# Sample stage of a fused decoder step: order of page loads, units of background work, matmul shapes, and a split last tile

## The chip, the cores and the metric

The kernel is one launch on one core of a Trainium2 chip. The time is the device time of that launch in microseconds; of several runs the median is given.

## What is computed

One layer for a prompt group (512 tokens) and a sample group (8 sequences of 8 new tokens with 1024 past positions in a paged cache), with shared weights. The part that the change touches, cut from the reference:

```python
# state-space branch (output side)
y = einsum('gcp,btgp->btgc', c_re, x_re) - einsum('gcp,btgp->btgc', c_im, x_im) + d * u
y = gelu(y.reshape(b, t, 512))
y_lin, y_gate = split(y @ w_glu, 2)
ssm_out = (y_lin * sigmoid(y_gate)) @ w_ssm_proj

# compression of cached keys and values, blocks of 32 rows with stride 16
hidden = gelu(lead[:, :-1] + trail[:, 1:] + pe_term + b1);  kc = hidden @ w2

# attention of the sample tokens: compressed blocks, selected blocks, window
o = gate[0] * o_c + gate[1] * o_s + gate[2] * o_w

# merge of the branches, then norm, router, experts
x = x + (sigmoid(g_s) * ssm_out + sigmoid(g_a) * (o @ w_attn_proj)) @ w_out
y = x + hier_moe(rms_norm(x, g_ffn))
```

The selection keeps 16 of 17 blocks, so the kernel masks the one block with the least score. Everything is float32.

## The kernel before

The program runs seven phases with a barrier of all engines between them: projection, building the state-space matrices, prompt attention, sample, merge, experts, combine. The change touches sample and merge.

**Sample.** The 8 sequences go two at a time through a loop of 4 iterations p. Each iteration on TensorE is: wide scores against window and cached keys (L1301 to L1308), the compressed keys and values (L1317, L1320), their scores (L1328), the sum over heads and the transposed probabilities (L1334, L1335), the compressed product (L1341), the compression of the next iteration's pages (`compress`, L1279), transposes of the probabilities (L1355) and two products with values, window then selected (L1373). ScalarE and VectorE evacuate, take softmaxes and run the selection, a chain of small VectorE steps (L1584 to L1604) between the head sum and the selected probabilities.

Between these steps stand nine points per iteration at which TensorE issues background work from a list that `background()` writes: state-space output units ("y", L1223 with 128 rows and L1225 with 64 rows, 8 of them, into PSUM banks 6 and 7), their transposes ("t", L1235), gated units ("g", L1246, 8 units of two halves e, each half an entry of its own) and the projection ("p", L1257, 16 of them). The work of entry n is evacuated by ScalarE and VectorE in `back_out(n + 1)`, a y unit's second half in `back_out(n + 2)`. START = 5 entries come ahead of the loop, entries behind point 36 after it. All y units are elementwise gelu on the way out: square (L1399), two VectorE steps (L1520, L1521), tanh (L1392), two VectorE steps (L1510, L1512).

Pages: SyncE issues one DMA per page of 128 KB, 16 per iteration, for the compressed slots into `pgc` (L1149; half of iteration 0 by ScalarE); GpSimd issues the other slots. `pgc` is single, so the pages of iteration p + 1 wait until `compress(p)` has read it (`cmp_ps`). SyncE also loads window keys and values (L1180, L1183), w_glu and w_ssm (L1186, L1187), which lie over matrices that the y units read, and the gates `sig_s` (L1193), all in one program order.

**Merge.** The attention projection (L1716), then for 5 row tiles (4 of 128 rows, the last of 64) the output projection in two halves of 512 columns (L1727, `out_ps`), the sum with x (L1806), the norm (L1774 to L1811), transposes (L1737) and router logits (L1743). Then the routing on VectorE and the expert loop, whose weights stream in: six pieces, 12 MB, are fetched ahead in merge, and each later one when the matmuls have used up its buffer.

## Time and profile before

| | |
|---|---|
| median of 3 runs | 1377.42 us (1375.86 to 1383.63) |
| profiled execution | 1375.69 us, span 1374.0 us |
| TensorE matmul | 1087.0 us busy, 79% of the span |
| VectorE, ScalarE, GpSimd | 391.6, 268.2, 236.5 us |
| mean granted clock | 0.876 |
| HBM | 284.27 MB read, 25.58 MB written |

From the page, the busy tenths in 40 equal slices of 34.35 us:

```profile
PE   5999997977789747789899966988778777777760
DVE  4446441657752322224342142000000000000005
PEclk9999998668875757889999976999999999999995
DMA  8321253130005044243065032999999999999946
```

Slices 13 to 20 are the sample stage, up to slice 24 merge and routing, then the expert loop. In timelines "idle before" is the time in which the engine did nothing ahead of the instruction, with what released it. Times are us from the start of the span.

### The profile page before, as it was taken

To read this page: it belongs to the slowest core of one execution; us is meant where nothing else is said; L and a number is where in the kernel's file an instruction comes from. 1 tells how busy PE (TensorE), PEld (TensorE's weight loads), DVE (VectorE), ACT (ScalarE), POOL (GpSimd) and SP (SyncE) were. 2 spreads that over 40 slices of the span, in tenths; PEclk is the share of its full clock that TensorE was granted. 3 is DMA by queue.
4 is the path that set the end of the run, shared out by engine and by line. 5 is a ranking of instruction groups with operands and counts; after the bars stand their busy time and mean duration, and the time that the engine had idled before them with its cause. 6 is when DMAs were issued, how large, how long until landed. Compare 5 with 4: busy or idle time off the path is not lost. (4 is left out here: it accounts for less than half of the span.)

```text
span 1374.0 us, 16631 instructions
## 1 busy us (share of the span) xinstructions
PE 1087.0 (79%) x5930; PEld 681.3 (50%) x5930; DVE 391.6 (29%) x957; ACT 268.2 (20%) x567; POOL 236.5 (17%) x604
## 2 busy tenths in 40 slices
PE   5999997977789747789899966988778777777760
PEld 5999997853346535557674433333222223223220
DVE  4446441657752322224342142000000000000005
ACT  5423222334431102111101110110100001111012
POOL 0007922088504001020000001010000000000010
PEclk9999998668875757889999976999999999999995
DMA  8321253130005044243065032999999999999946
GB/s 333 108 92 63 87 183 89 38 134 1 5 0 189 27 184 163 75 154 146 1 265 216 26 141 104 421 421 420 421 421 421 421 422 421 421 421 421 420 195 221
DMA packets 71256, 299.30 MB, mean 218 GB/s; under 512 B 12086, under 2 KB 30390, under 8 KB 44694
## 3 DMA queue, kind: packets, MB, share of 16 engines
q1 hardware_dynamic: 60750, 274.79, 50.5%
q0 software_dynamic: 9296, 22.71, 4.6%
q10 hardware_dynamic: 1152, 1.05, 0.3%
q8 instruction: 34, 0.56, 0.2%
q14 instruction: 24, 0.20, 0.0%
HBM read 284.27 MB, written 25.58 MB: 226 GB/s over the span
## 5 line engine op out<-in xcount | busy, mean ns | idle before, releaser
L2020 PE MATMUL ps<-arena,local_late 128*64 128x512 f32 x1280 | 308.5, 630 | 99.7 <-DMA arena<-in_w_exp 80.6
L2020 PEld LDWEIGHTS ps<-arena,local_late 128*64 128x64 f32 x1280 | 101.7, 144 | 294.8 <-issue 273.1
L349 PE MATMUL ps<-local_project 128*128 128x288 f32 (+4 forms) x1608 | 205.2, 290 | 17.6 <-DVE local_project L488 16.8
L349 PEld LDWEIGHTS ps<-local_project 128*128 128x128 f32 (+1 forms) x1608 | 204.3, 184 | 18.1 <-DVE local_project L488 16.8
L2068 DVE SCALAR_TENSOR_TENSOR arena<-arena,ps 128x512 f32<-128x512 f32 x16 | 11.0, 688 | 306.6 <-ACT arena L2052 306.6
L1149 POOL DMA_DIRECT2D local_sample<-in_cache x64 | 35.1, 549 | 215.2 <-issue 215.2
L1727 PE MATMUL ps<-local_late,arena 128*128 128x512 f32 (+1 forms) x160 | 69.6, 594 | 1.0 <-DVE arena L1797 1.0
L1990 POOL TENSOR_TENSOR arena<-arena 1x1 f32<-1x1 f32 x16 | 2.9, 183 | 350.4 <-ACT local_late L2060 350.4
L2044 ACT ACTIVATE local_late<-ps 128x512 f32<-128x512 f32 x34 | 18.5, 594 | 221.3 <-PE ps L2003 221.3
L1246 PE MATMUL ps<-arena 128*128 128x288 f32 x128 | 43.1, 490 | 18.5 <-DVE arena L1526 18.5
L2071 DVE SCALAR_TENSOR_TENSOR arena<-arena,ps 128x512 f32<-128x512 f32 x16 | 11.0, 688 | 163.9 <-PE ps L2020 163.9
L2020 PE MATMUL ps<-local_late 128*64 128x512 f32 x256 | 57.7, 592 | 0.0
L389 DVE TENSOR_TENSOR local_project<-arena,local_project 128x2048 fp32r<-128x2048 f32 (+1 forms) x15 | 35.4, 2361 | 66.5 <-ACT local_project L301 66.5
L1279 PE MATMUL ps<-arena 128*128 128x128 f32 x256 | 33.7, 299 | 18.8 <-DMA arena<-in_cache 18.8
L1727 PEld LDWEIGHTS ps<-local_late,arena 128*128 128x128 f32 (+1 forms) x160 | 28.4, 179 | 39.5 <-issue 37.9
L891 PE MATMUL ps<-local_prompt 64*128 64x128 f32 (+3 forms) x128 | 31.1, 581 | 19.8 <-ACT local_prompt L951 18.9
L1279 PEld LDWEIGHTS ps<-arena 128*128 128x128 f32 x256 | 33.0, 214 | 20.0 <-DMA arena<-in_cache 19.2
L1246 PEld LDWEIGHTS ps<-arena 128*128 128x128 f32 x128 | 27.7, 227 | 28.1 <-DVE arena L1526 19.9
L2060 ACT ACTIVATE local_late<-ps 128x512 f32<-128x512 f32 x32 | 19.1, 597 | 105.5 <-PE ps L2020 105.5
L1257 PE MATMUL ps<-arena 128*128 128x288 f32 x128 | 35.1, 424 | 3.5 <-DVE arena L1533 3.5
L1970 POOL MEMSET arena<- 1x8 f32 x1 | 0.1, 95 | 217.8 <-POOLq L2208 217.8
L951 ACT ACTIVATE local_prompt<-ps,local_prompt 128x128 f32<-128x128 f32 (+3 forms) x64 | 33.0, 521 | 21.8 <-DVE local_prompt L1007 21.7
(377 smaller groups left out, 1405.4 us busy)
## 6 DMA issues: line engine op xcount, KB each, us to landing
arena<-in_w_exp SPq DMA_DIRECT2D x160, 1024.0 KB, 25.3
local_late<-in_w_exp SPq DMA_DIRECT2D x32, 1024.0 KB, 25.5
arena<-in_w_rest SPq DMA_DIRECT2D x9, 1024.0 KB, 5.7
local_sample<-in_cache POOLq DMA_DIRECT2D x64, 128.0 KB, 3.1
arena<-in_cache SPq DMA_DIRECT2D x56, 128.0 KB, 3.8
arena<-in_w_wide SPq DMA_DIRECT2D x6, 1040.0 KB, 5.2
scratch_sig<-arena POOLq DMA_DIRECT2D x16, 288.0 KB, 2.6
arena<-scratch_sig SPq DMA_DIRECT2D x2, 2304.0 KB, 9.5
```

What stands on the lines that cost most here:

```text
L349: mm = pe.matmul(out, stationary(s, k), moving(m, k), start=k == 0 and a == 0, stop=k == KD - 1 and a == 2)
L389: dve.tensor_tensor(W[:, n % 2, 1, :, 0:width], raw[:, n % 2, :, 0:width], W[:, n % 2, 0, :, 0:width].bitcast(F32), ALU.subtract).then_inc ...
L891: mm = pe.matmul(c.ps[:, t % 2 * 2 + g, 0:n], qT[HD * g:HD * (g + 1), h, i * P:(i + 1) * P], kT[HD * g:HD * (g + 1), s, 0:n], start=True, ...
L951: ins = act.activation(pr[:, s, g, h, 0:n], c.ps[:, t % 2 * 2 + g, 0:n], ACT.Exp, bias=bias[:, t % 4, g:g + 1], scale=-1.0, accum_out=tota ...
L1149: eng.dma_start(dst[:, a], c.d["cache"][bass.ds(v, 1)].rearrange("o p s e -> (o p) s e")[:, parts]).then_inc(arrived, 16)
L1246: mm = pe.matmul(c.ps[:, 6 + e, 0:HALF], w_glu[:, k, (4 * e + j) * P:(4 * e + j + 1) * P], yT[:, k, t], start=k == 0, stop=k == 3)
L1257: mm = pe.matmul(c.ps[:, 6 + u % 2, 0:HALF], w_ssm[:, k, m * P:(m + 1) * P], glu[:, k, t], start=k == 0, stop=k == 3)
L1279: mm = pe.matmul(c.ps[:, 4, (s * 2 + g) * P:(s * 2 + g + 1) * P], c.w1[:, s, j], mov, start=j == 0, stop=j == 7)
L1727: mm = pe.matmul(c.ps[0:ROWS[i], n, :], sig_a[:, k, i * P:i * P + ROWS[i]], w_out[:, k, n * 512:(n + 1) * 512], start=k == 0, stop=k == KD ...
L2020: mm = pe.matmul(c.ps[SLOTS * q:SLOTS * (q + 1), bank, :], tokens[:, k0 + k, SLOTS * q:SLOTS * (q + 1)], raw[p][q][:, k], start=first and ...
L2044: act.activation(XT[:, 4 * a:4 * a + 4], c.ps[:, a, :].rearrange("p (k t) -> p k t", k=4), ACT.Copy).then_inc(xt_out, 1)
L2060: act.activation(Y[:, h * 512:(h + 1) * 512], c.ps[:, 6 + h, :], ACT.Copy).then_inc(y_out, 1)
```

## The change

- The background list has 4 y units instead of 8, each with both halves (64-row parts side by side in two banks, banks 6/7, 0/1, 2/3, 6/7), and whole gated units at every other entry instead of halves at every entry. The second (gate) half comes first, so that ScalarE can start on it.
- The order ahead of the loop is y 0, y 1, compression 0, y 2, y 3.
- Y units are evacuated whole in `back_out(n + 1)`; for VectorE one `back_out` moves into the selection chain, ahead of the masking.
- SyncE loads the pages of iteration 1 ahead of w_glu and w_ssm, and window keys and values of iteration 1 ahead of the gates.
- The compression multiplies 256 columns at once instead of twice 128.
- In merge, the last row tile's two column halves go to different output partitions (0 to 63 and 64 to 127) of two banks, alternating; ScalarE copies the second half down to partitions 0 to 63 before VectorE adds it.

```diff
-    y = [[("y", n)] for n in range(8)]
+    y = [[("y", n)] for n in range(4)]
     turn = [[("t", n), ("t", n + 1)] for n in range(0, 8, 2)]
-    glu = [[("g", u, e)] for u in range(8) for e in range(2)]
+    glu = [part for u in range(8) for part in ([("g", u)], [])]
...
+        Y_BANK = [6, 0, 2, 6]
...
-            pages(sp, 0, pgc, slice(0, 2), cmp_in, range(PAGES))
-            for p in range(NP):
+            def window(p):
                 if p:
                     sp.wait_ge(wide_ps, p)
                 sp.dma_start(wk[:], c.d["win_kT"][:, 2 * p:2 * p + 2]).then_inc(wk_in, 16)
                 if p:
                     sp.wait_ge(pv_ps, 3 * (p - 1) + 2)
                 sp.dma_start(wv[:], c.d["win_v"][:, 2 * p:2 * p + 2]).then_inc(wv_in, 16)
-                if p == 0:
-                    sp.wait_ge(y_ps, 8)
-                    sp.dma_start(w_glu[:], c.d["w_glu"]).then_inc(wg_in, 16)
-                    sp.dma_start(w_ssm[:], c.d["w_ssm"]).then_inc(ws_in, 16)
-                if p + 1 < NP:
-                    sp.wait_ge(cmp_ps, p + 1)
-                    pages(sp, p + 1, pgc, slice(0, 2), cmp_in)
-                if p == 0:
-                    sp.wait_ge(yt_ps, 8)
-                    sp.dma_start(sig_s[:], c.d["sig"][0:8].rearrange("m p t -> p m t")).then_inc(ss_in, 16)
+
+            def next_pages(p):
+                sp.wait_ge(cmp_ps, p)
+                pages(sp, p, pgc, slice(0, 2), cmp_in)
+
+            pages(sp, 0, pgc, slice(0, 2), cmp_in, range(PAGES))
+            window(0)
+            next_pages(1)
+            sp.wait_ge(y_ps, 8)
+            sp.dma_start(w_glu[:], c.d["w_glu"]).then_inc(wg_in, 16)
+            sp.dma_start(w_ssm[:], c.d["w_ssm"]).then_inc(ws_in, 16)
+            window(1)
+            sp.wait_ge(yt_ps, 8)
+            sp.dma_start(sig_s[:], c.d["sig"][0:8].rearrange("m p t -> p m t")).then_inc(ss_in, 16)
+            for p in range(2, NP):
+                next_pages(p)
+                window(p)
...
-                        if u >= 2:
-                            pe.wait_ge(y_done, u - 1)
+                        if u == 1:
+                            pe.wait_ge(small_out, 3)
+                        if u == 3:
+                            pe.wait_ge(y_done, 2)
                         for a in range(4):
-                            g = 2 * (4 * (u // 2) + a) + u % 2
-                            lo, tl = HD * (g % 2), g // 2
-                            out = c.ps[0:NCH, 6 + u % 2, a * P:(a + 1) * P]
-                            pe.matmul(out, c.U[:, g], c.KT[:, :, g * 16:(g + 1) * 16], start=True, stop=False)
+                            out = [c.ps[0:NCH, Y_BANK[u] + h, a * P:(a + 1) * P] for h in range(2)]
+                            tl = 4 * u + a
+                            for h in range(2):
+                                g = 2 * tl + h
+                                pe.matmul(out[h], c.U[:, g], c.KT[:, :, g * 16:(g + 1) * 16], start=True, stop=False)
                             for r in range(2):
-                                mm = pe.matmul(out, c.XM[lo:lo + HD, r, tl], c.C[lo:lo + HD, r, tl].rearrange("p t e -> p (t e)"),
-                                               start=False, stop=r == 1)
-                        mm.then_inc(y_ps, 1)
+                                for h in range(2):
+                                    rows = slice(HD * h, HD * (h + 1))
+                                    mm = pe.matmul(out[h], c.XM[rows, r, tl], c.C[rows, r, tl].rearrange("p t e -> p (t e)"),
+                                                   start=False, stop=r == 1)
+                                    if a == 3 and r == 1:
+                                        mm.then_inc(y_ps, 1)
...
-                        e, j, t = unit[2], u // 2, slice(u % 2 * HALF, (u % 2 + 1) * HALF)
-                        if u == 0 and e == 0:
+                        j, t = u // 2, slice(u % 2 * HALF, (u % 2 + 1) * HALF)
+                        if u == 0:
                             pe.wait_ge(yt_out, 8)
                             pe.wait_ge(wg_in, 16)
-                        if u >= 1 and e == 0:
+                        else:
                             pe.wait_ge(glu_done, u)
-                        for k in range(4):
-                            mm = pe.matmul(c.ps[:, 6 + e, 0:HALF], w_glu[:, k, (4 * e + j) * P:(4 * e + j + 1) * P],
-                                           yT[:, k, t], start=k == 0, stop=k == 3)
-                        mm.then_inc(glu_ps, 1)
+                        for e in (1, 0):
+                            for k in range(4):
+                                mm = pe.matmul(c.ps[:, 6 + e, 0:HALF], w_glu[:, k, (4 * e + j) * P:(4 * e + j + 1) * P],
+                                               yT[:, k, t], start=k == 0, stop=k == 3)
+                            mm.then_inc(glu_ps, 1)
...
-                    for g in range(2):
-                        for j in range(8):
-                            mov = pgc[:, :, s].rearrange("p a (g j n) -> p a g j n", g=2, j=8)[:, :, g, j]
-                            mm = pe.matmul(c.ps[:, 4, (s * 2 + g) * P:(s * 2 + g + 1) * P], c.w1[:, s, j], mov,
-                                           start=j == 0, stop=j == 7)
+                    out = c.ps[:, 4, s * 2 * P:(s + 1) * 2 * P].rearrange("p (g a n) -> p a g n", g=2, n=8)
+                    for j in range(8):
+                        mov = pgc[:, :, s].rearrange("p a (g j n) -> p a g j n", g=2, j=8)[:, :, :, j]
+                        mm = pe.matmul(out, c.w1[:, s, j], mov, start=j == 0, stop=j == 7)
...
-            for n in range(START - 1):
+            back_step(0)
+            back_step(1)
+            compress(0)
+            for n in range(2, START):
                 back_step(n)
-            compress(0)
-            back_step(START - 1)
             pe.wait_ge(small_out, 3)
             pe.wait_ge(qb_zero, 9)
+            pe.wait_ge(y_done, 6)
...
+                        for h in range(2):
+                            act.wait_ge(y_ps, 2 * u + h + 1)
+                            if u:
+                                act.wait_ge(y_tanh, 2 * u + h - 1)
+                            act.activation(tmp[0:NCH, h, 0], c.ps[0:NCH, Y_BANK[u] + h, :], ACT.Square).then_inc(sq_done, 1)
+                        for h in range(2):
+                            act.wait_ge(u_ready, 2 * u + h + 1)
+                            if u:
+                                act.wait_ge(y_done, 2 * u + h - 1)
+                            act.activation(tmp[0:NCH, h, 1], tmp[0:NCH, h, 0], ACT.Tanh, scale=GELU_B).then_inc(y_tanh, 1)
...
-            for n in range(START - 1):
+            for n in range(2):
                 back_out(n)
             for g in range(2):
                 r = slice(HD * g, HD * (g + 1))
                 for h in range(HG):
                     act.activation(qb[r, :, g, h], qs[r, h].rearrange("p (b t) -> p b t", b=NB), ACT.Copy).then_inc(qb_zero, 1)
-            back_out(START - 1)
+            back_out(2)
             trail_rows(0)
             hidden_tanh(0)
+            for n in range(3, START):
+                back_out(n)
...
-            for n in range(START):
+            for n in range(3):
                 back_out(n)
             hidden(0)
+            for n in range(3, START):
+                back_out(n)
...
                 link(dve.tensor_scalar(b17[:, 3], b17[:, 2], s1[:, 13:14], NEG, ALU.is_equal, ALU.mult))
+                back_out(point(p, 3))
...
-                for k in range(3, 7):
+                for k in range(4, 7):
...
-                if i < TILES:
+                if i < TILES - 1:
                     for n in range(2):
                         if i >= 1:
                             pe.wait_ge(x_done, 2 * i + n - 1)
@@ -1727,6 +1745,14 @@
                             mm = pe.matmul(c.ps[0:ROWS[i], n, :], sig_a[:, k, i * P:i * P + ROWS[i]],
                                            w_out[:, k, n * 512:(n + 1) * 512], start=k == 0, stop=k == KD - 1)
                         mm.then_inc(out_ps, 1)
+                if i == TILES - 1:
+                    pe.wait_ge(x_done, 2 * i)
+                    for k in range(KD):
+                        for n in range(2):
+                            mm = pe.matmul(c.ps[64 * n:64 * (n + 1), n, :], sig_a[:, k, SEQ:TOK],
+                                           w_out[:, k, n * 512:(n + 1) * 512], start=k == 0, stop=k == KD - 1)
+                            if k == KD - 1:
+                                mm.then_inc(out_ps, 1)
...
+                if i == TILES - 1:
+                    act.wait_ge(out_ps, 2 * TILES)
+                    act.activation(moved[:], c.ps[64:P, 1, :], ACT.Copy).then_inc(half_moved, 1)
...
-                    dve.tensor_tensor(xs, c.ps[0:r, n, :], xs, ALU.add).then_inc(x_done, 1)
+                    term = c.ps[0:r, n, :]
+                    if i == TILES - 1 and n == 1:
+                        dve.wait_ge(half_moved, 1)
+                        term = moved[:]
+                    dve.tensor_tensor(xs, term, xs, ALU.add).then_inc(x_done, 1)
```

The evacuation of a y unit on VectorE has the same steps as before, for h = 0 and h = 1, and counts `y_ps`, `u_ready`, `y_tanh` and `y_done` by halves.

## Rows read from the trace of the kernel before

**Rows 1.** Busy time by stage: stretch, length, then busy time (instructions), clock, DMA.

```profile
414.40:689.40 275.00, 214.58 (x1206) 156.66 (x1206) 84.15 (x228) 45.57 (x127) 35.11 (x64) 0.78 0.34 117
689.40:840.80 151.40, 124.55 (x448) 75.14 (x448) 49.05 (x121) 14.40 (x29) 4.22 (x7) 0.89 0.38 149
840.80:1374.00 533.20, 394.53 (x1786) 149.35 (x1786) 42.02 (x57) 62.55 (x114) 45.33 (x98) 0.92 0.94 386
```

**Rows 2.** Groups by line and shape, whole kernel: busy, mean ns, idle before.

```profile
L1246 PE MATMUL ps<-arena 128*128 128x288 f32 x128 | 43.1, 490 | 18.5 <-DVE arena L1526 18.5
L1257 PE MATMUL ps<-arena 128*128 128x288 f32 x128 | 35.1, 424 | 3.5 <-DVE arena L1533 3.5
L1279 PE MATMUL ps<-arena 128*128 128x128 f32 x256 | 33.7, 299 | 18.8 <-DMA arena<-in_cache 18.8
L1225 PE MATMUL ps<-arena 64*72 64x128 f32 x128 | 33.2, 406 | 0.0
L1223 PE MATMUL ps<-arena 128*72 128x128 f32 x64 | 20.5, 420 | 8.1 <-DVE arena L1512 8.1
L1235 PE MATMUL ps<-arena 72*128 72x72 f32 x32 | 4.5, 312 | 4.9 <-ACT arena L1403 2.5 <-DVE arena L1512 2.4
```

**Rows 3.** SyncE's waits in 410 to 680 us: total, times, longest.

```profile
SPq L1186 <- PE ps L1225: 64.3, 1, 64.3
```

**Rows 4.** Timeline of SyncE's queue: start, duration of issuing, instruction.

```profile
488.79 0.33 SPq L1186 DMA_DIRECT2D arena<-in_w_glu  x1
...
490.35 17.26 SPq L1149 DMA_DIRECT2D arena<-in_cache  x16
533.03 0.40 SPq L1193 DMA_DIRECT2D arena<-scratch_sig  x1
533.47 0.58 SPq L1180 DMA_DIRECT2D arena<-in_win_kT  x1
...
587.79 16.85 SPq L1149 DMA_DIRECT2D arena<-in_cache  x16
```

**Rows 5.** Timeline of TensorE: start, busy, instruction, idle before.

```profile
453.26 0.38 PE L1223 MATMUL ps<-arena 128*72 128x128 f32 x2
...
457.02 0.34 PE L1301 MATMUL ps<-local_sample 128*64 128x64 f32 x4
...
509.45 9.19 PE L1279 MATMUL ps<-arena 128*128 128x128 f32 x64 [18.81 <-DMA arena<-in_cache]
...
543.81 0.42 PE L1301 MATMUL ps<-local_sample 128*64 128x64 f32 x4 [4.45 <-issue]
...
565.97 4.21 PE L1246 MATMUL ps<-arena 128*128 128x288 f32 x8 [6.19 <-DVE arena L1526]
...
677.72 9.97 PE L1257 MATMUL ps<-arena 128*128 128x288 f32 x40
```

**Rows 6.** Timeline of TensorE in prompt attention, 64-row scores on alternating row halves.

```profile
371.63 1.99 PE L891 MATMUL ps<-local_prompt 64*128 64x512 f32 x8
```

**Rows 7.** Busy time and clock of two stretches, columns as in rows 1.

```profile
416.00:443.00 27.00, 27.00 (x98) 17.12 (x99) 8.10 (x20) 5.62 (x17) 12.79 (x24) 0.50 0.71 224
...
640.00:660.00 20.00, 19.16 (x127) 12.80 (x125) 11.09 (x35) 3.58 (x14) 0.00 (x0) 1.00 0.54 216
```

**Rows 8.** Timeline, evacuation of a y unit: its first and last step.

```profile
423.88 0.59 ACT L1399 ACTIVATE local_sample<-ps 72x512 f32<-72x512 f32 x1
...
427.94 0.69 DVE L1512 TENSOR_TENSOR arena<-ps,local_sample 72x512 f32<-72x512 f32 x1
```

**Rows 9.** Timeline of the last row tile in merge and of the first experts.

```profile
787.83 13.95 PE L1727 MATMUL ps<-local_late,arena 128*64 128x512 f32 x32
...
801.81 0.68 DVE L1806 TENSOR_TENSOR arena<-ps,arena 64x512 f32<-64x512 f32 x1 [6.18 <-PE ps L1727]
...
806.51 0.97 PE L1737 MATMUL ps<-arena,local_late 64*128 64x64 f32 x8 [1.00 <-DVE local_late L1811]
...
844.76 15.39 PE L2020 MATMUL ps<-arena,local_late 128*64 128x512 f32 x64 [1.37 <-ACT local_late L2044]
```

50 lines of the change are left out of this document (19 added, 31 removed).

## Prediction

> **What bounds the kernel now.** I read the busy table by stage first. The sample stage (414.4 to 689.4 us) lasts 275.0 us with TensorE busy for 214.6 of them, the merge stage 151.4 us, and the expert loop with the tail 533.2 us at 386 GB/s, DMA share 0.94 [rows 1]. The last of these is bound by reading expert weights: its length does not depend on when it begins, since its transfers start only as its own matmuls release buffers, and the six pieces that are fetched ahead are fetched in merge. So a microsecond taken from sample or merge is a microsecond of the whole, and in both TensorE is the engine that everything follows. The second view, the groups by line with shapes kept apart, says what its 275 us are: gated units (L1246) 43.1 us busy and 18.5 idle before them, projections (L1257) 35.1 and 3.5, compression (L1279) 33.7 and 18.8, state-space output (L1225 and L1223) 33.2 + 20.5 = 53.7 and 8.1, its transposes (L1235) 4.5 and 4.9, and the wide scores (L1301) have 4.45 before them [rows 5]. Together these are 58 of the 60.4 us in which TensorE is idle. The third view is the clock: 0.50 through the first 27 us of state-space output although TensorE never paused, and 1.00 in 640 to 660 us [rows 7]. A projection group of 8 instructions costs 9.97 / 5 = 1.99 us at the full clock, and the same shape 4.21 us in the stretch that follows a 6.19 us pause [rows 5].
>
> **The change, part by part.**
>
> *Pages ahead of weights.* SyncE stands 64.3 us until the last state-space unit is out [rows 3]. Only then, at 488.79 us, do w_glu and w_ssm go out and, behind them, the 16 pages of iteration 1, at 1.05 us of issuing each (17.26 us) [rows 4]. TensorE wants them at 490.6 and gets them at 509.45: 18.8 us idle [rows 2, 5]. The change lets these pages go when compression 0 has ended (about 444 us, below), so they are issued by 461 and are there before compression 1 can start (477). The 18.8 us go entirely. What is late next is the chain of small steps ahead of compression 1. The window keys of iteration 1 are now issued before the gates: before, they stood behind 2.3 MB of gates (533.03, 533.47) and landed for a start at 543.81, so these 4.4 us go too [rows 4, 5]. New on SyncE: the wait for the window product of iteration 0 (window values 1) now holds back the gates and the pages of iteration 2. It ends at about 492 by my walk, pages 2 are in by 515, and compression 2 wants them at about 523: hidden by 8 us. Pages 3 start after the window product of iteration 1, as before (587.79) [rows 4], but the iterations are shorter: about 2 to 4 us of cover are left. That is a rival.
>
> *State-space output in row halves.* A unit now holds both halves: 16 instructions over 128 rows and 32 over 64 rows, where before two units held the same 48. The halves sit on different rows and in different banks. The row for such pairs is the prompt's 64-row scores: 8 instructions of 512 columns in 1.99 us, 0.25 each [rows 6], where 512 columns alone cost 13.95 / 32 = 0.44 each [rows 9]. So 32 cost what 16 did: 32 instruction times a unit in place of 48. An instruction time is 53.7 / 192 = 0.28 us on average, nearly all at half clock [rows 2], and (457.02 - 453.26) / 24 = 0.157 at full clock [rows 5]. Two units before compression 0 at half clock, 9.0 us each, and two behind it at full clock, 5.0 each (before, the clock was full behind compression 0 too), give 28 in place of 53.7 us: -25.7. Bounds: no pairing gives 13.5 and 7.5, so 14 us more; full clock from the start, 8 us less. The 8.1 us of waits for banks 6 and 7 go, as units 1 and 2 write banks 0 to 3. In their place stands one wait: evacuating a unit, from square to product, took 423.88 to 428.63 for one half [rows 8], some 5.5 us for two, and transposes and score reads stand behind that of unit 3: 3 us idle beside the wide scores.
>
> *Turns inside iteration 0.* The 8 transposes now lie in the softmax chain of iteration 0 where four output units lay, and alternate with ScalarE's copies, which stand behind that iteration's own ScalarE work. By walking the three queues instruction by instruction compression 1 starts at 477 (before 509.45), with about 4 us idle among them, near the 4.9 us that they had [rows 2]. The last two copies stand behind the trail rows of compression 1, so the first gated unit waits 2 us.
>
> *Whole gated units, cleared mid-chain.* Work is unchanged: 16 groups of gating, 16 of projection, 1.99 us each at the full clock, 31.8 us a kind. Before, 43.1 + 35.1 were spent; the excess of 14.6 is slow clock behind pauses [rows 2]. The pauses of 18.5 come from a unit whose clearing lay behind the selection chain of VectorE (6.19 the longest [rows 5]). A unit is now issued only at every other point, so its clearing has a whole point to itself, and for the projections the one before is cleared inside the chain. What remains: about 1 us at each score read, 2 at the softmax of iterations 0 and 1 where no group covers it any longer, 1 for the product with its predecessor: 4.3 us in iteration 1, 2 in iteration 2, 1.5 in 3, 2.8 in the rest of 0. As eight y units became four, the background list ends inside iteration 3: the four projections behind the loop (of 9.97 us for five [rows 5]) move into iterations 0 to 2 and are no longer alone at the end. Slow clock: I leave 2 of the 14.6 in place for gating and none for projection, and add 5 us below for it.
>
> *Compression 256 wide.* 32 instructions in place of 64 for the same columns. At full clock 128 columns cost about 0.116, and 288 columns 9.97 / 40 = 0.249, so 256 should cost 0.22: 0.4 us saved each time, -1.7 together. The loads were hidden already. A dearer pattern of reading is not seen in any row; bounds -2 and +3.
>
> *Last tile split.* The 64 rows of tile 4 took 13.95 us for 32 instructions [rows 9]. With its two halves on different columns they should run as the experts' do, 64 in 15.39 us, 0.24 each [rows 9]: 7.7 us, -6.2. Both halves now end together, so the added copy (a similar one took 0.59 [rows 8]) and one sum that was hidden (0.68 [rows 9]) stand on the path, and the copy behind tile 3's evacuation: about 4.4 of the 6.2 reach the start of the last transposes at 806.51 [rows 9]. Bounds: -5.5 and, if the columns don't pair, +1.4.
>
> *The sum.* Busy: output 28, gating 34, projection 32, compression 32, and the rest, 214.6 - 53.7 - 43.1 - 35.1 - 33.7 = 49.0, about 46: 172 us. Idle: start 1.7, output 3, turns 4, rest of iteration 0 4.8, iterations 4.3 + 2 + 1.5, end 2: 23. With 5 for slow clock behind the new short pauses: 200 us. The walk along the order of instructions, with each semaphore's own delay, gives 208. I take 206: -69. With the tile -73. The profiled execution is 1375.7 us (span 1374.0) against a median of 1377.4; 1377.4 - 73 = 1304.
>
> **The rivals.**
>
> *Output units dearer than priced* (1317): pairs don't form or loads show, 8 to 14 us more. Against it stands the prompt's row [rows 6]; for it, that the 64-row pairs there are 4 times as wide. The Trainium skill, "TensorE: Matmul & The Clock Gate", Part 3, says both that matmuls on different row groups run together and that a weight load overlaps only matmuls of other row groups. By the second half, the 16 full-height loads of a unit would stand open; whatever loads stand open in the kernel before already lie inside my 0.28 us, and my bound of 14 us holds the rest.
>
> *Pages 3 late* (1314): compression 3 waits on a queue that issues 16.85 us of pages [rows 4] in an iteration that has become 17 us shorter; 5 to 12 us, with the slow clock that follows a pause. By the Trainium skill, "DMA: Bandwidth & Descriptors", Issuing engines are not separate DMA queues, issuing is usually small beside the transfer; the row says the opposite here, 1.05 us to issue 128 KB. If the page held, this rival would have no chance.
>
> *Fuller clock* (1291): with fewer pauses the clock rises in the first output units and stays up: 8 us from output, 5 from my allowance.
>
> *Slower than before* (1400): the stage runs at half clock. The new order bunches transposes and short products in iteration 0 and leaves whole points uncovered; if the clock then stayed at 0.50, the 150 us of the sum that I price at full would double (4.21 for 1.99 [rows 5]). The change breaks even when some 70 of the 150 run so. Against it: 640 to 660 us, the same mix with pauses, stood at 1.00 [rows 7]; for it: 0.50 through 27 us of unbroken output [rows 7].
>
> *The time doesn't reach the end* (1350 to 1375): the expert loop waits for something that merge now reaches too early. The pieces fetched ahead are 12 of 1 MB in 151 us at 149 GB/s [rows 1], so there is room.
>
> **How the numbers follow.** Forecast 0.72, dearer output 0.09, late pages 0.07, fuller clock 0.07, slower 0.02, not reaching the end 0.03. The forecast's own range, from the bounds of compression (5), tile (6), pauses (8) and output (6), is 1292 to 1320. The range, which takes in the dear and the fuller case, is 1286 to 1331. A change under 0.5% can't be told from none here. Faster by more: 0.97; within: 0.01; slower: 0.02.
>
> **What would show it.** No idle before the compression of iteration 1; sample stage about 206 us; a state-space unit of 8 to 9 us at half clock and 5 at full; pauses before gated units under 5 us in all; the last projection before the loop's end; clock of the stage near 0.9; tile 4 in 7.7 us; expert loop and tail still 533 us. A long DMA-ended pause before compression 2 or 3, or a clock of 0.5 past 480 us, would make the prediction wrong.

## The result and the profile after

The kernel after takes 1284.22 us (median of 4 runs, 1283.38 to 1285.02), the kernel before 1376.64 us beside it (4 runs, 1375.79 to 1383.63). The ratio is 0.9316, 95% interval 0.9295 to 0.9337: 92 us or 6.8% faster. The forecast was 1304 us and its range ended at 1286, so the kernel came out 20 us faster than forecast and just below the range.

The busy table by stage of the kernel after (stretch, length, then busy time and instructions of TensorE, its weight loads, VectorE, ScalarE and GpSimd, the granted clock, the DMA share, GB/s), to be read against [rows 1]:

```profile
415.80:602.30 186.50, 167.35 (x1078) 124.39 (x1078) 83.17 (x228) 46.03 (x127) 35.02 (x64) 0.94 0.51 173
602.30:749.50 147.20, 118.71 (x452) 74.09 (x453) 49.07 (x121) 15.11 (x30) 4.22 (x7) 0.87 0.41 153
749.50:1283.30 533.80, 393.48 (x1784) 148.17 (x1782) 42.06 (x57) 62.55 (x114) 45.32 (x98) 0.93 0.94 385
```

The sample stage went from 275.0 to 186.5 us, merge from 151.4 to 147.2, and the expert loop with the tail, 533.8 us, kept its length and began earlier. With a start that is 1.4 us later, these make -90.7 us, which is the difference of the spans (1374.0 and 1283.3). In the sample stage TensorE's busy time fell by 47.2 us with 128 instructions fewer, all of them in compression, and its idle time fell from 60.4 to 19.2. The mean granted clock of the stage rose from 0.78 to 0.94.

The groups by line and shape (busy us, mean ns | idle before them), which answer to [rows 2]. L1271 is projection, L1260 gating, L1293 compression, L1237 and L1233 the state-space output over 64 and 128 rows:

```profile
L1271 PE MATMUL ps<-arena 128*128 128x288 f32 x128 | 36.3, 429 | 1.9 <-DVE arena L1547 1.1 <-DVE arena L1540 0.8
L1260 PE MATMUL ps<-arena 128*128 128x288 f32 x128 | 33.0, 411 | 4.3 <-DVE arena L1540 2.4 <-ACT arena L1416 2.0
L1293 PE MATMUL ps<-arena 128*128 128x256 f32 x128 | 30.5, 399 | 0.0
L1237 PE MATMUL ps<-arena 64*72 64x128 f32 x128 | 11.5, 302 | 0.0
L1233 PE MATMUL ps<-arena 128*72 128x128 f32 x64 | 11.4, 305 | 0.7 <-ACT arena L1467 0.7
```

State-space output is 22.9 us where it was 53.7, compression waits for nothing (18.8 before), gating waits 4.3 (18.5 before). Projection alone is no cheaper (36.3 for 35.1). A second profile of the same kernel (the yardstick below) has 36.4 us of gating in place of 33.0, at equal pauses, so 3.4 us of slow clock come and go there between executions.

TensorE's timeline from the first output unit to the first gated unit (start, busy, instruction, idle before it), which answers to [rows 5] and [rows 7]:

```profile
418.31 1.13 PE L1233 MATMUL ps<-arena 128*72 128x128 f32 x4
419.37 1.13 PE L1237 MATMUL ps<-arena 64*72 64x128 f32 x8
...
422.51 0.66 PE L1233 MATMUL ps<-arena 128*72 128x128 f32 x4
423.09 0.66 PE L1237 MATMUL ps<-arena 64*72 64x128 f32 x8
...
425.66 0.66 PE L1233 MATMUL ps<-arena 128*72 128x128 f32 x4 [0.72 <-ACT arena L1467]
...
430.37 7.17 PE L1293 MATMUL ps<-arena 128*128 128x256 f32 x32
...
451.84 0.72 PE L1248 MATMUL ps<-arena 72*128 72x72 f32 x8 [1.30 <-DVE arena L1532]
...
455.31 1.26 PE L1248 MATMUL ps<-arena 72*128 72x72 f32 x8 [1.20 <-ACT arena L1416]
...
461.33 1.27 PE L1248 MATMUL ps<-arena 72*128 72x72 f32 x8 [0.93 <-ACT arena L1416]
...
463.16 8.94 PE L1293 MATMUL ps<-arena 128*128 128x256 f32 x32
474.07 4.15 PE L1260 MATMUL ps<-arena 128*128 128x288 f32 x16 [1.96 <-ACT arena L1416]
```

Two things are to be seen. At 422.5 us, inside the first output unit, a group falls from 1.13 to 0.66 us: the clock has risen, where before it stayed at 0.50 for 27 us of the same work [rows 7]. And the 8 instructions of the 64-row group take what 4 of the 128-row group take, 1.13 us at half clock and 0.66 at full: the two halves run side by side. Compression 1 starts at 463.16, where before it started at 509.45 [rows 5]. The clock did not stay up all the way: among the turns, with pauses of 0.9 to 1.5 us, it was lower again (columns as in rows 1), and compression 1 began slow, 8.94 us for the 7.17 of compression 0.

```profile
451.80:463.10 11.30, 7.31 (x55) 5.98 (x55) 5.10 (x22) 5.12 (x13) 1.09 (x2) 0.56 0.88 308
```

SyncE's queue (start, duration of issuing), which answers to [rows 4]:

```profile
438.28 17.21 SPq L1149 DMA_DIRECT2D arena<-in_cache  x16
455.54 0.80 SPq L1193 DMA_DIRECT2D arena<-in_w_glu  x1
...
482.89 16.85 SPq L1149 DMA_DIRECT2D arena<-in_cache  x16
...
526.16 17.36 SPq L1149 DMA_DIRECT2D arena<-in_cache  x16
```

The pages of iteration 1 go out as compression 0 ends, and the weights behind them. The pages of iteration 3 are all issued at 543.5; compression 3 starts at 548.06 and waits for nothing.

The split tile, TensorE's timeline in merge, against [rows 9]:

```profile
700.71 7.09 PE L1752 MATMUL ps<-local_late,arena 128*64 128x512 f32 x32
...
714.09 1.11 PE L1763 MATMUL ps<-arena,local_late 64*128 64x64 f32 x8 [2.55 <-DVE local_late L1844]
```

From its first matmul to its last transposes it takes 13.4 us, where it took 18.7.

**Where the 20 us are.** I cut the sample stage of both traces at the same instructions:

| from .. to | before, us | after, us | change | prediction |
|---|---|---|---|---|
| start .. compression 1 | 95.0 | 47.3 | -47.7 | -32 |
| compression 1 .. wide scores of iteration 1 | 34.4 | 30.0 | -4.4 | not stated |
| iteration 1 | 55.8 | 38.8 | -17.1 | -17 |
| iteration 2 | 46.3 | 38.5 | -7.8 | not stated |
| iteration 3 and end | 43.5 | 31.9 | -11.6 | not stated |

The right-hand column holds what the prediction states of the walk that gave 208 us. Of the 21.5 us between 208 and the measured 186.5, about 16 lie in the first row: the walk was 8.8 us too dear in output units and compression 0, and 7.0 us too dear between the last output unit and compression 1. From compression 1 to compression 2 it had 46 us (477 to 523) and the trace has 46.8 (463.16 to 509.96), and iteration 1 came as it said. Where the other 5 or 6 us lie can't be told, as the prediction doesn't state its other parts.

### The profile page after: what moved, and what is told of

Read it like the earlier page. It is cut to its first block and busy times, and to the rows that moved or that the text cites. A ratio compares the mean times of both kernels' runs of the same rounds, so it can differ in the third digit from the quotient of the medians.

```text
span 1283.3 us, 16387 instructions
## 1 busy us (share of the span) xinstructions
PE 1033.2 (81%) x5802; PEld 647.7 (50%) x5802; DVE 391.0 (30%) x957; ACT 268.9 (21%) x568; POOL 236.5 (18%) x604
## 3 DMA queue, kind: packets, MB, share of 16 engines
q10 hardware_dynamic: 1152, 1.05, 0.3%
## 5 line engine op out<-in xcount | busy, mean ns | idle before, releaser
L349 PE MATMUL ps<-local_project 128*128 128x288 f32 (+4 forms) x1608 | 205.7, 290 | 18.0 <-DVE local_project L488 17.2
L349 PEld LDWEIGHTS ps<-local_project 128*128 128x128 f32 (+1 forms) x1608 | 204.7, 185 | 18.5 <-DVE local_project L488 17.2
L2077 ACT ACTIVATE local_late<-ps 128x512 f32<-128x512 f32 x34 | 18.4, 595 | 220.6 <-PE ps L2036 220.6
L1745 PE MATMUL ps<-local_late,arena 128*128 128x512 f32 x128 | 55.7, 594 | 1.0 <-DVE arena L1826 1.0
L1745 PEld LDWEIGHTS ps<-local_late,arena 128*128 128x128 f32 x128 | 24.1, 190 | 30.7 <-issue 29.2
L2085 ACT ACTIVATE arena<-ps 128x512 f32<-128x512 f32 x16 | 9.6, 597 | 137.5 <-PE ps L2053 137.5
L1271 PE MATMUL ps<-arena 128*128 128x288 f32 x128 | 36.3, 429 | 1.9 <-DVE arena L1547 1.1
L853 PEld LDWEIGHTS ps<-arena,local_prompt 128*128 128x128 f32 x160 | 23.9, 180 | 26.6 <-DVE local_prompt L982 13.8
L2053 PEld LDWEIGHTS ps<-local_late 128*64 128x64 f32 x256 | 18.6, 137 | 36.3 <-issue 36.1
L1260 PE MATMUL ps<-arena 128*128 128x288 f32 x128 | 33.0, 411 | 4.3 <-DVE arena L1540 2.4
L1007 DVE CUSTOM_DVE_ANT_0 ps<-ps,local_prompt 128x128 f32<-128x128 f32 (+3 forms) x64 | 30.2, 513 | 20.6 <-PE ps L891 20.4
```

The lines of the kernel that those rows point to most:

```text
L349: mm = pe.matmul(out, stationary(s, k), moving(m, k), start=k == 0 and a == 0, stop=k == KD - 1 and a == 2)
L853: mm = pe.transpose(c.ps[:, 4 + g, h * P:(h + 1) * P], pr[:, s, g, h, a * P:(a + 1) * P], c.k("ident"))
L1007: ins = dve.tensor_tensor_reduce(S, S, mask[:, SEQ - n:SEQ], -SCALE, 3.0e38, ALU.add, ALU.min, bias[:, t % 4, g:g + 1])
L1260: mm = pe.matmul(c.ps[:, 6 + e, 0:HALF], w_glu[:, k, (4 * e + j) * P:(4 * e + j + 1) * P], yT[:, k, t], start=k == 0, stop=k == 3)
L1271: mm = pe.matmul(c.ps[:, 6 + u % 2, 0:HALF], w_ssm[:, k, m * P:(m + 1) * P], glu[:, k, t], start=k == 0, stop=k == 3)
L1745: mm = pe.matmul(c.ps[0:ROWS[i], n, :], sig_a[:, k, i * P:i * P + ROWS[i]], w_out[:, k, n * 512:(n + 1) * 512], start=k == 0, stop=k == KD ...
```

## The experiments

Each kernel is the kernel after with one thing undone or varied, but for the third and fourth, which are the kernel before with one thing added. The edits are shown as sketches: `U, g` stands for the product over 128 rows, `XM, C of half h` for one over 64 rows, and lines that only follow the edit are left out. Times stand beside 1284.22 us of the kernel after, which gave 1284.41 in the third group of runs (the yardstick, below). The medians carry intervals of 0.15 to 0.4% of the kernel before, so a difference of 2 us between two kernels is not measured by its median; where one matters it is read from the timeline. The kernel before, run beside each group, had medians of 1376.6 to 1382.0 us, so the ratios compare better than the times. The start of the sample stage varies too, although nothing ahead of it was changed: the first output product starts between 414.7 and 420.9 us in these profiles. So timelines of two kernels are compared from that product on.

**1. The two halves one after the other.** Each half finishes its four tiles before the other starts; banks, places and waits stay.

```
-for a in range(4):
-    for h in range(2): U, g
-    for r in range(2):
-        for h in range(2): XM, C of half h
+for h in range(2):
+    for a in range(4):
+        U, g
+        for r in range(2): XM, C of half h
```

> The changed kernel with one edit: inside a state-space unit all products of the first half come ahead of all products of the second, so that no two neighbouring 64-row matmuls lie on different rows. Theory A (the pairs, and with them the denser work, raised the clock in the first unit): units 0 and 1 at the half clock as before the change, 13.4 us each, compression 0 about 9 us, units 2 and 3 7.6 us each behind it; the wide scores start 50 to 52 us after the first unit instead of 29.2; about 1306 us. Theory B (the clock rises in the first unit whatever the order, pairing only shortens the instructions): four units of 7.6 us and 7.2 for the compression, 37.6 us, about 1293 us. Theory C (pairing does nothing): as the changed kernel, 1284 us.

Measured: 1305.31 us, ratio 0.9472 (0.9457 to 0.9488), +21. Busy table and clock of units 0 and 1, and of units 2 and 3 behind compression 0:

```profile
417.00:444.00 27.00, 27.00 (x99) 17.12 (x98) 6.82 (x18) 4.88 (x16) 12.73 (x23) 0.50 0.70 224
454.30:469.30 15.00, 15.00 (x96) 9.87 (x95) 9.16 (x17) 4.21 (x8) 0.00 (x0) 1.00 0.39 114
```

The first 27 us are those of the kernel before to the microsecond, at 0.50 with TensorE busy without a pause. Behind compression 0 the same work runs at 1.00 in 15.0 us. So the order of the 48 instructions of a unit made the clock rise early. But the edit changes two things at once: the halves no longer stand side by side, and the shape changes four times a tile instead of twice. Experiments 10 to 12 take that up. One other explanation falls here: more instructions in the same time. The clock rose inside compression 0, between 448 and 450 us, and there TensorE had run 6 recorded instructions in 2 us (446 to 448), fewer in a microsecond than the 99 in 27 us of output.

**2. The weights ahead of the pages again.**

```
 window(0)
-next_pages(1)
 sp.wait_ge(y_ps, 8)
 ...w_glu, w_ssm
-window(1)
+next_pages(1)
 ...sig_s
+window(1)
```

> The changed kernel with SyncE's order of before: weights of the gated units ahead of the pages of iteration 1, gates ahead of the window of iteration 1. Theory A (the stall was the wait for the last state-space unit, not the weights' bytes): that unit now ends at 447, so the pages are issued 448 to 465 and compression 1 starts at about 467 instead of 463: +4 us, about 1288 us. Rival (the order itself was worth the stall of 18.8 us and the 4.4 us before the wide scores): +20 us or more, 1304 us or above.

Measured: 1291.75 us, 0.9369 (0.9351 to 0.9386), +7.5. TensorE's timeline:

```profile
470.21 8.05 PE L1293 MATMUL ps<-arena 128*128 128x256 f32 x26 [6.77 <-DMA arena<-in_cache]
```

The pages were late by 6.8 us, not by the 18.8 of before, as the four output units now end sooner. From the first output product to compression 1 it is 51.1 us, for 44.9 in the kernel after. The queue's order is worth some 7 us in the new kernel, more than the 4 that I expected, and the rival's 20 did not come.

**3. The pages ahead of the weights, alone, in the kernel before.** The new order of SyncE's queue, and nothing else.

> The kernel before with SyncE's new order alone. Theory A: the stall of 18.8 us and the 4.4 us before the wide scores of iteration 1 go and nothing takes their place: -23 us, about 1354 us; compression 1 starts at about 491. Rival (the evacuation of the last output units and the transposes behind it take part of the place of the stall): -12 to -18 us, 1359 to 1365 us.

Measured: 1349.93 us, 0.9789 (0.9773 to 0.9806), -27.8. The gated units of this kernel:

```profile
L1252 PE MATMUL ps<-arena 128*128 128x288 f32 x128 | 41.6, 477 | 18.5 <-DVE arena L1532 18.5
```

The wait before compression 1 is gone, and the pauses of gating are untouched, 18.5 us as in [rows 2]. I had priced the two stalls at 23.2 us. By the profiled spans the edit gives 25.4 (1374.0 to 1348.6), or 26.9 from the first output product on, which came 1.5 us later in this profile. Of the 3.7 us above the two stalls, 1.5 are gating at a fuller clock (43.1 to 41.6); where the rest lies I haven't followed.

**4. The paired output alone.** The kernel before with output in row halves and the shorter list of units; weights ahead of pages, gating in halves, nothing cleared mid-chain, compression 128 wide, last tile whole. Of the new gating only the order of the two halves is kept.

> The changed kernel with everything but the four double output units and their place reverted: SyncE's order, gated units by halves at every point, no clearing inside the selection chain, compression by 128 columns, last tile whole. Theory A (the units and the clock are the larger part): what is reverted costs 4 (order), 4.4 (tile), 1 (compression), 6 (gated units and clearing) us: about 1300 us. Rival (the whole gated units carry the 18.5 us of waits that stood before L1246): those come back, 1315 to 1320 us.

Measured: 1319.27 us, 0.9565 (0.9535 to 0.9594). Groups by line (L1259 is gating, L1270 projection), then the timeline at compression 1:

```profile
L1259 PE MATMUL ps<-arena 128*128 128x288 f32 x128 | 38.0, 443 | 18.4 <-DVE arena L1540 16.4 <-ACT arena L1416 2.0
L1270 PE MATMUL ps<-arena 128*128 128x288 f32 x128 | 36.9, 434 | 5.7 <-DVE arena L1547 3.5 <-DVE arena L1540 2.1
```

```profile
470.25 9.54 PE L1292 MATMUL ps<-arena 128*128 128x128 f32 x64 [6.79 <-DMA arena<-in_cache]
```

Of the 92 us, 58 come with this part. The shorter list does not take the pauses before gated units away (18.4 us), so it is the whole gated units that took them away (experiment 5). My theory, by which most of them would go with the list, fell here.

**5. Gating in halves, clearing mid-chain kept.**

```
-glu = [part for u in range(8) for part in ([("g", u)], [])]
+glu = [[("g", u, e)] for u in range(8) for e in (1, 0)]
```

> The changed kernel with gated units issued by halves at every point, as before the change, but with the clearing inside the selection chain kept. Theory A (the waits before L1246 came from a unit that is issued one point after its predecessor's second half, with the selection chain between them): the waits before gated units, 4.3 us now, return to 10 to 14 us, less than the 16.4 us of the run with no clearing in the chain, since the clearing now comes in its middle; about 1293 us. Rival (clearing in mid-chain alone cured them): waits stay under 6 us, 1285 us.

Measured: 1296.31 us, 0.9395 (0.9362 to 0.9428), +12.1.

```profile
L1259 PE MATMUL ps<-arena 128*128 128x288 f32 x128 | 40.0, 463 | 15.4 <-DVE arena L1539 13.5 <-ACT arena L1415 2.0
```

The pauses are back, a little above what I expected (15.4 for 4.3), and gating is busy 7.0 us longer (40.0 for 33.0). Some 5 of the 7 are slow clock in four groups of eight, the slowest 3.90 us for 2.21, each right behind a pause of 1.8 to 3.4 us. But 36.4 also occur in the kernel after, so how much of the 7 this edit brings is known to a few microseconds only. Projection is 1.7 us cheaper, which is the one slow group of the kernel after (3.90 for 2.21 at 541.64) at full clock.

**6. Nothing cleared mid-chain.** VectorE clears the unit of point 3 behind the selection chain again.

```
-back_out(point(p, 3))
 ...S, s1[:, 14:15], s1[:, 4:5]
-for k in range(4, 7):
+for k in range(3, 7):
```

> The changed kernel with the one clearing moved back behind the selection chain. Theory A (whole units at every other point never have their clearing behind the chain, only the projections of iteration 3 do): the wait of 3.5 us before a projection in iteration 3 returns in place of 1.1, about +2.5 us, 1287 us. Rival (the mid-chain clearing carries the gated units too): +8 us or more, 1292 us.

Measured: 1289.77 us, 0.9360 (0.9325 to 0.9395), +5.5, between the 2.5 that I expected and the rival's 8. Groups by line, then the timeline in iteration 3:

```profile
L1271 PE MATMUL ps<-arena 128*128 128x288 f32 x128 | 38.6, 450 | 4.3 <-DVE arena L1547 3.5 <-DVE arena L1540 0.8
```

```profile
585.09 4.21 PE L1271 MATMUL ps<-arena 128*128 128x288 f32 x8 [3.54 <-DVE arena L1547]
```

Gating is untouched (33.0 us busy, 4.3 idle): an empty point follows each gated unit, so its clearing needs no room inside the chain. What the edit costs is one pause of 3.54 us among the projections of iteration 3 and the clock behind it (4.21 for 2.21), which I had not priced. Iteration 3 is 5.0 us longer by it: 2.4 more idle before projections, 2.3 more busy in them, and a small rest behind them.

**7. The last tile whole.**

```
-if i < TILES - 1:
+if i < TILES:
```

(with the split branch, ScalarE's copy and its wait removed)

> The changed kernel with the last row tile whole. Both traces show 18.7 us from the tile's first matmul to the last transposes before the change and 13.4 us after it; so +5.2 us, about 1289.5 us. Rival (a neighbour of the tile gives it back: the router's chain or the row store ends last anyway): +0 to +2 us.

Measured: 1292.17 us, 0.9359 (0.9321 to 0.9396), +8.0. TensorE's timeline in merge:

```profile
706.65 13.95 PE L1745 MATMUL ps<-local_late,arena 128*64 128x512 f32 x32
...
725.34 0.73 PE L1755 MATMUL ps<-arena,local_late 64*128 64x64 f32 x8 [1.00 <-DVE local_late L1830]
```

13.95 us and 18.7 to the last transposes, as before: the split is worth 5.3 us. The rest of the 8 us is not the tile's. In this profile the tile begins 5.9 us later than in the kernel after, although nothing ahead of it was changed: 2.6 us of it are already there at the first output product, and 3.4 are gating, busy 36.4 us for 33.0. The yardstick, which is the kernel after itself, shows the same 36.4, in the same two units (5.84 us for 4.15, the first and the fourth). So the clock differs there between executions of one kernel; why stays open.

**8. Compression 0 behind all four output units.** It asks whether compression, the wide dense product, is what keeps the clock up for units 2 and 3.

```
-back_step(0); back_step(1); compress(0)
-for n in range(2, START): back_step(n)
+for n in range(START): back_step(n)
+compress(0)
```

> The changed kernel with compression 0 behind all four state-space units. Theory A (paired units alone raise and hold the clock): granted clock 1.0 in units 2 and 3 without a compression ahead of them, the four units end at about 440, the wide scores start where they did, and the pages of iteration 1, which wait for compression 0, come 9 to 10 us later, so compression 1 starts at about 467: +4 us, 1288 us. Theory B (the compression between them held the clock up): units 2 and 3 fall to 0.5 and take 8.4 us each instead of 4.7: +7 us more, 1295 us.

Measured: 1285.52 us, 0.9333 (0.9297 to 0.9370), +1.3. Busy table of units 2 and 3, then the timeline at compression 1:

```profile
427.00:440.00 13.00, 13.00 (x119) 9.83 (x116) 12.29 (x25) 7.92 (x20) 6.01 (x11) 1.00 0.53 183
```

```profile
463.79 8.40 PE L1293 MATMUL ps<-arena 128*128 128x256 f32 x29 [2.59 <-DMA arena<-in_cache]
```

The units ran at 1.00 with no compression ahead of them. The pages of iteration 1 wait for compression 0 and so arrive 2.6 us late. The stage began 2.7 us earlier in this profile; from the first output product to compression 1 it is 48.1 us, for 44.9 in the kernel after, so 3.3 us later, near the 4 expected. The median, +1.3, is too coarse for that.

**9. Compression 128 wide.**

```
-for j in range(8): out 256 wide, both g
+for g in range(2):
+    for j in range(8): out 128 wide
```

> The changed kernel with the compression by 128 columns. Four compressions of 64 instructions: at full clock 7.4 us instead of 7.17 each; +1 us in all, 1285 us, not to be told from the changed kernel by its time, only by the group's busy time (31.5 against 30.5 us). Rival (each dropped weight load was open): +3.7 us each, 1299 us.

Measured: 1285.98 us, 0.9318 (0.9286 to 0.9351), +1.6. All compression is busy 31.7 us there in 256 recorded instructions, and 30.5 us in 128 in the kernel after: the width is worth 1.2 us, for the 1.7 priced.

**The yardstick.** The kernel after once more, beside experiments 9 to 11.

> The changed kernel itself, again, as the yardstick of this chip: 0.9316 of the kernel before, stage of 186.5 us, first output unit at half clock for 4 us and all others at full.

Measured: 1284.41 us, 0.9311 (0.9285 to 0.9336). The group that differs from the profile shown at first:

```profile
L1260 PE MATMUL ps<-arena 128*128 128x288 f32 x128 | 36.4, 442 | 4.3 <-DVE arena L1540 2.4
```

The time is the same within its interval, though gating is busy 3.4 us longer.

**10. Only unit 0 in pairs.** Units 1 to 3 as in experiment 1.

> The changed kernel with paired products in state-space unit 0 only; units 1 to 3 in the unpaired order. Theory A (the pairs raise the clock, and once up it stays up in the unpaired order too, as it did for units 2 and 3 of the fully unpaired run): clock 1.0 from the first unit's second half on, units 1 to 3 cost 7.6 us each instead of 4.7, compression 0 7.2: +8.7 us, about 1293 us. Rival (the clock needs the pairs throughout): it falls back to 0.5 in unit 1, which takes 13 us, and compression 0 starts at half: +17 us or more, 1301 us.

Measured: 1290.81 us, 0.9358 (0.9334 to 0.9383), +6.4. Busy table of the first 5 us of unit 0, then of 27 us in which lie unit 1, compression 0 and most of units 2 and 3:

```profile
417.00:422.00 5.00, 5.00 (x29) 3.72 (x29) 0.00 (x0) 0.00 (x0) 2.41 (x5) 0.52 0.91 273
425.00:452.00 27.00, 27.00 (x159) 19.17 (x158) 18.41 (x40) 9.74 (x24) 13.06 (x24) 1.00 0.69 221
```

The clock rose inside unit 0 and the three unpaired units stayed at 1.00, without a pause. Once it is up, unpaired work keeps it; what experiment 1 lacked was the rise.

**11. The halves grouped.** Per tile both products over 128 rows, then both of the lower half, then both of the upper.

```
-for r in range(2):
-    for h in range(2):
+for h in range(2):
+    for r in range(2):
```

> The changed kernel with the 64-row products of a tile grouped by half: both 128-row products, then the two state products of the first half, then those of the second. The changes of shape are as few as in the changed kernel, but only one pair of neighbours per tile lies on different rows. Theory A (work side by side on both halves raised the clock): clock 0.5 through units 0 and 1, about 11 to 12 us each, compression 0 about 9: some +17 us, 1301 us. Theory B (fewer changes of shape, and so fewer pauses of the weight loads, raised it): clock 1.0 from unit 0 on, units of 5 to 6.5 us, +3 to +8 us, 1288 to 1292 us.

Measured: 1284.03 us, 0.9311 (0.9285 to 0.9338), the same as the kernel after. Busy table, then two groups of unit 0:

```profile
417.00:421.00 4.00, 4.00 (x24) 2.88 (x24) 0.00 (x0) 0.00 (x0) 2.07 (x4) 0.50 0.89 268
421.00:445.00 24.00, 23.71 (x203) 18.06 (x200) 17.48 (x39) 10.13 (x26) 11.06 (x21) 1.00 0.76 245
```

```profile
421.15 0.67 PE L1233 MATMUL ps<-arena 128*72 128x128 f32 x4
421.76 0.67 PE L1237 MATMUL ps<-arena 64*72 64x128 f32 x8
```

I had expected the halves to run one after the other here and the clock to stay low. It rose, and for a moment that spoke for the rival, fewer changes of shape. The rows say why it does not: 8 instructions of 64 rows still take 0.67 us, so the halves ran side by side all the same. Neighbours need not alternate strictly; the four instructions of the upper half ran beside the four of the lower that stood ahead of them. The experiment had not taken away what it was meant to.

**12. Same shapes, one half.** The alternation of the kernel after (two products over 128 rows, four over 64), but all four on the same half: two tiles take the place of the two halves. The results land in the places of other tiles, so this kernel doesn't compute the layer; it serves for its times alone. Units 0 and 2 do the lower half, units 1 and 3 the upper.

```
-tl = 4 * u + a; out[h]: half h of tile tl
+h = u % 2; tls = [8 * (u // 2) + 2 * b + i for i in range(2)]; out[i]: half h of tile tls[i]
```

> The kernel after, with the state-space output in the same alternation of shapes as there (two pieces of 128 rows, then four of 64 rows), but the four of 64 rows all on the same half: two tiles of the same half take the place of the two halves of one tile (units 0 and 2 do the lower half, units 1 and 3 the upper). The results land in the places of other tiles, so the output is not the reference's; the instructions are the same in number and shape. Theory A, the two halves side by side are what raised the clock: units 0 and 1 stay at 0.50, as in the unpaired kernel; a unit then takes 2 x 1.13 us for the 128 rows' and the 64 rows' blocks twice as long as in the kernel after (4 x (1.13 + 2.1) = 13 us), units 2 and 3 about 7.0 us each at full, and the kernel takes 1303 us or a little less. Theory B, fewer changes of shape raised it (two a tile instead of four): the clock rises inside unit 0 as in the kernel after (by 424), the 64 rows' blocks still take twice the time, 4 x (0.59 + 1.17) = 7.0 us a unit at full against 4.7, so 4 x 2.35 = 9.4 us more plus about 1 in the slow part: 1294 us. Busy time of the 64 rows' groups: 28 us or more by A, about 20 by B.

Measured: 1297.26 us, 0.9405 (0.9379 to 0.9431), +13.0. Busy table of units 0 and 1, and of units 2 and 3, then the timeline:

```profile
417.00:439.40 22.40, 22.40 (x92) 17.72 (x91) 5.70 (x16) 4.55 (x16) 10.39 (x20) 0.50 0.75 240
448.60:461.40 12.80, 12.80 (x97) 10.17 (x95) 8.04 (x15) 3.71 (x8) 1.64 (x3) 1.00 0.48 143
```

```profile
416.79 1.98 PE L1238 MATMUL ps<-arena 64*72 64x128 f32 x8
418.70 1.13 PE L1235 MATMUL ps<-arena 128*72 128x128 f32 x4
...
450.74 1.09 PE L1238 MATMUL ps<-arena 64*72 64x128 f32 x8
```

The shape changes exactly as often as in the kernel after, TensorE is busy without a pause, and the clock stays at 0.50 through both units. So the halves side by side raised the clock, not the grouping of shapes. The time alone would not have told: 1297 lies between the two expectations, because I had priced a unit at half clock at 13 us and it took 11.9. The clock column tells, and so does the time from the first output product to the wide scores: 45.7 us, for 29.2 in the kernel after and 51.5 in experiment 1. Of the 22 us between those two, 4 x (7.6 - 4.7) = 12 are the unpaired work at full clock, and the rest is the clock. What side by side changes that the clock answers to, a fuller array or more products in the same time, these runs don't separate.

**The parts add up.** Undone one at a time in the kernel after, the queue's order, whole gated units, mid-chain clearing, width and tile cost 7.5 + 12.1 + 5.5 + 1.6 + 8.0 = 34.7 us; experiment 4, which lacks all five, is 35.1 us above it. By ratios to the kernel before of the same group, the five make 31 us and experiment 4 34. With some 2 us of uncertainty in each of them, this leaves no room for a large interaction among the five. Pairing does interact, with the queue's order: together they removed the 18.8 us, of which the order alone would take all and pairing alone 12. No version tried is measurably faster than the kernel after.

## Why the prediction was right and where it was wrong

*What bounds the kernel: right.* A microsecond of the sample stage was a microsecond of the whole. Expert loop and tail took 533.8 us for 533.2 though they began 91 us earlier, and the case "the time doesn't reach the end" is out.

*Pages ahead of weights: right.* Both stalls are gone, none took their place, and experiment 3 gives 27 to 28 us for 23.2. In the whole kernel the order is worth 7 (experiment 2), because pairing takes 12 of the same 18.8 us. Pages 3 were all issued at 543.5, and a page takes a median of 3.0 us from issue to landing in this stage, so an estimated 1.5 us or more was left until 548.06, near the 2 to 4 that the prediction gave. The Trainium skill's page "DMA: Bandwidth & Descriptors", Issuing engines are not separate DMA queues, has issuing as usually small beside the transfer. Here 16 pages occupy SyncE for 17.2 us, 1.08 each (the prediction's 1.05 is that of the 16.85 us group): a third of the 3.0 us of one page. But the 16 transfers overlap and their issues don't, so issuing sets the time of the whole (in experiment 2 they were issued from 448.9 to 468.5, and compression 1 started at 470.2), and a queue's order remains worth watching.

*State-space output: mechanism right, size wrong, and this is the step that failed.* I priced two units at 9.0 us (half clock) and two at 5.0, 28 us, and compression 0 at half clock. The price at full clock was good (4.7 for 5.0). Wrong was the clause "two units before compression 0 at half clock". It rested on [rows 7], where the clock stood at 0.50 through the same products; but that row was taken with the halves one after the other, and the change ends just that. Units and compression 0 took 28.5 us (418.31 to 446.8) in place of 37.3 (2 x 9.0 + 9.3 + 2 x 5.0, with compression 0 at the 9.3 us of before), 8.8 less: 5.9 in units 0 and 1, 2.3 in compression 0, 0.6 in units 2 and 3. Experiments 1 and 12 show that side by side is the condition, 8 that compression is not, 10 that the clock then stays. The prediction's "fuller clock" rival had the mechanism ("the clock rises in the first output units and stays up: 8 us from output, 5 from my allowance"), and got a chance of 0.07. Its sizes are only near: 6.5 us came from output and 2.3 from compression 0, which it doesn't name, and the clock fell again among the turns (0.56 from 451.8 to 463.1).

*Turns inside iteration 0: the second mis-sized term.* The walk was given only by its result, 477. From the last output unit to compression 1 it was 16.3 us and not 23.3 (454 to 477). By my account, which the recorded prediction doesn't show, each of the eight turns of output stood in the walk at 1.27 us, which is what one entry of eight instructions takes: two turns. [rows 2] had the answer, 32 instructions in 4.5 us; 8 x 1.27 - 4.5 = 5.7 of the 7.0 are this. The idle time among them was about 5 us for the 4 given, and the first gated unit waited 1.96 for 2.

*Gating, projection, clearing.* Gating was 33.0 us for 34 and all its pauses with those of projection 6.2 us; experiment 5 shows the cause as the prediction has it. Projection was priced too low: 36.3 for 32. Of the 4.3, 1.7 are one slow group (3.90 for 2.21 at 541.64). The rest is the price itself: 1.99 us is the mean of five groups in a row, and a group that stands among other work shows 2.10 to 2.21, 15 of the 16 here. The 5 us for slow clock stood beside these terms; what slow clock there was, 1.7 here and 1.8 in compression 1, lies inside the busy terms of the measured stage. By groups: busy 167.4 for 172, idle 19.2 for 23, allowance 0 for 5, which is 186.5 for 200. The 6 us by which I went from 200 toward the walk's 208 were an error of the walk: without the 7 us of the turns it gives 201.

*Compression and tile.* Compression got 1.2 us cheaper by width, for 1.7. The tile took 7.1 us for 7.7, and 5.3 of it reached the last transposes for 4.4.

*The range.* Its lower end took in the fuller clock (1291) but not that clock together with an error in the walk: 1304 - 13 - 6 = 1285, with 1284 measured. The sum by groups at 200 and the walk at 208 were a sign of that error; I went most of the way to the walk instead of looking for it. That the sum by groups came nearer is in part luck: projection too low by 4.3 hid as much of what was too high.

## What to carry to other kernels

A granted clock belongs to the order of instructions in which it was recorded; if the change alters which products run side by side, price the work at both levels and ask what would decide between them. Where two ways of adding up the same stage differ by more than the range's own terms, look for the instruction count that differs, before the mean is taken. An order of transfers that removes a stall is worth that stall only while the work ahead of it keeps its length.

## What the runs showed of the hardware

- **A busy TensorE need not get the full clock.** It stayed at 0.50 (the lower of its two levels, 1.2 and 2.4 GHz) through 27.0 us of pauseless work in experiment 1 and 22.4 us in experiment 12, and rose at 422.5 us, inside the first unit, in the same products with the two row halves side by side. Once up, it stayed at 1.00 through unpaired units (15.0 us in experiment 1, experiment 10). The Trainium skill, "TensorE: Matmul & The Clock Gate", Part 1, describes the clock as released by sustained activity and taken back by idleness. If activity is read as TensorE being busy, the trace of experiment 1 does not agree: 27.0 of 27.0 us busy, at 0.50.
- **Halves run side by side even when they are not strict neighbours.** 8 instructions of 64 rows took 0.66 us alternating and 0.67 in groups of four per half (experiment 11), but 1.09 on one half (experiment 12). The Trainium skill, "TensorE: Matmul & The Clock Gate", Part 3, says that matmuls on different row groups run together, and the trace agrees.
- **Weight loads overlapped full-height matmuls.** The Trainium skill, "TensorE: Matmul & The Clock Gate", Part 3, also says that a weight load overlaps only matmuls of other row groups. Compression fills all 128 rows, so its loads have no other group to overlap; yet in the kernel before its matmuls and its loads (second and third figure) were both recorded busy for the whole of 5.00 us, at 45 each. Could a load not run beside a matmul of its own rows, the two would take turns, and neither could be busy all the time. At full clock 64 of them take 7.41 us, 0.116 each, loads included. The trace doesn't agree with that sentence.

```profile
448.00:453.00 5.00, 5.00 (x45) 5.00 (x45) 0.00 (x0) 0.00 (x0) 2.24 (x5) 0.97 0.36 116
...
621.07 7.41 PE L1279 MATMUL ps<-arena 128*128 128x128 f32 x64
```

- **A change of shape costs little.** The unpaired unit took 7.6 us at full clock with four changes a tile (experiment 1) and 6.4 with two (experiment 12). If the eight changes are all that differs, one costs some 0.15 us, an estimate.
